# One ones product per norm, named activation tables, one-column bank marks, and another order at the ends of the feed-forwards and in the gated mixing

## The reference

```python
def rmsnorm(x, g):                       # called for every norm
    y = x * lax.rsqrt(jnp.mean(x * x, axis=-1, keepdims=True) + EPS)
    return y * g

def conv_ffn(h, w_up, conv_w, conv_b, w_down):        # ffn0
    up = jnp.pad(h @ w_up, ((0, 0), (1, 1), (0, 0)))
    u = sum(up[:, j:j + t] * conv_w[j] for j in range(3)) + conv_b
    a, g = jnp.split(u, 2, axis=-1)
    return (jax.nn.gelu(a) * g) @ w_down

def swiglu_ffn(h, w_in, w_out):                       # ffn1 to ffn4
    gate, up = jnp.split(h @ w_in, 2, axis=-1)
    return (jax.nn.silu(gate) * up) @ w_out

def gmlp_chunk_mix(h, w_uv, v_norm, w_s, b_s, w_o):   # mix2
    u, v = jnp.split(jax.nn.gelu(h @ w_uv), 2, axis=-1)        # 2048 wide each
    v = rms_norm(v, v_norm).reshape(B, 2, 128, 16, 128)        # 2 chunks, 16 groups
    sv = einsum('gts,bcsgd->bctgd', causal(w_s), v) + b_s      # a 128x128 product per group and chunk
    return (u * sv.reshape(B, S, 2048)) @ w_o

# first block: h = norm(x) @ w_in -> hgrn2 scan (two directions, with log of a sigmoid),
#   neighbourhood attention, attention on mem; gated sum @ w_out; conv_ffn; norm
# second block: ffn1, rwkv7, xattn, ffn2, ffn3, gmlp mix2, xattn, ffn4, final norm
```

## Time and profile before

| | before |
|---|---|
| median of 3 runs | 1980.64 us |
| the profiled execution's own time | 1974.38 us |
| its span (first to last instruction) | 1972.2 us |
| TensorE busy | 1886.9 us, 96% |
| TensorE weight loads | 1786.0 us, 91% |
| VectorE busy | 1407.4 us, 71% |
| ScalarE busy | 1044.1 us, 53% |
| GpSimd busy | 45.7 us, 2% |
| read from memory | 310.5 MB, 158 GB/s over the span |

### The profile page before, as it was taken

One profiled execution on the slowest core, in us unless ns is written; L12 is line 12 of the kernel. 1 busy time (PEld: TensorE's weight loads), 2 busy tenths in 40 slices (PEclk: granted clock), 3 DMA queues, 4 the chain that ended last, 5 costly groups with the idle time before them and its releaser, 6 DMA issues. The chain is left out here.

```text
span 1972.2 us, 40546 instructions
## 1 busy us (share of the span) xinstructions
PE 1886.9 (96%) x16839; PEld 1786.0 (91%) x16844; DVE 1407.4 (71%) x1786; ACT 1044.1 (53%) x1390; POOL 45.7 (2%) x42
## 2 busy tenths in 40 slices
PE   7999998999999999989987999999999998999998
PEld 7998997999998899989886999998999998999997
DVE  6685589767777877798565667778777756557776
ACT  6565576755556444568533554445444555545443
POOL 0000000000000000000052000000000000000000
PEclk9999999999999999999999999999999999999999
DMA  6843333354553455444401434554455453534552
GB/s 219 251 175 127 129 129 113 128 187 172 190 192 139 160 195 188 171 146 149 154 4 46 150 127 173 191 189 174 172 190 192 168 190 117 182 113 174 189 192 107
DMA packets 52316, 313.39 MB, mean 159 GB/s; under 512 B 13536, under 2 KB 13792, under 8 KB 14944
## 3 DMA queue, kind: packets, MB, share of 16 engines
q1 hardware_dynamic: 51760, 308.42, 44.2%
q10 hardware_dynamic: 432, 3.15, 0.4%
HBM read 310.50 MB, written 1.05 MB: 158 GB/s over the span
## 5 line engine op out<-in xcount | busy, mean ns | idle before, releaser
L2138 DVE TENSOR_TENSOR wl<-raw,wh 128x1024 fp32r<-128x1024 f32 x576 | 687.5, 1223 | 375.7 <-ACT wh L1462 372.8
L1462 ACT ACTIVATE wh<-raw 128x1024 fp32r<-128x1024 f32 x575 | 587.8, 1051 | 304.2 <-PE ps L308 154.8
L308 PE MATMUL ps<-pages_r,wh 128*128 128x256 f32 x2480 | 548.1, 287 | 34.1 <-DVE wl L2138 17.7
L308 PE MATMUL ps<-pages_r,wl 128*128 128x256 f32 x1680 | 479.0, 285 | 0.0
L308 PEld LDWEIGHTS ps<-pages_r,wh 128*128 128x128 f32 x2480 | 424.8, 195 | 38.8 <-issue 19.1
L308 PE MATMUL ps<-norm_r,wh 128*128 128x256 f32 x2336 | 430.2, 285 | 2.5 <-DVE norm_r L2202 1.7
L308 PEld LDWEIGHTS ps<-norm_r,wh 128*128 128x128 f32 x2336 | 365.9, 192 | 5.6 <-issue 2.0
L372 PE MATMUL ps<-norm_r,wh 128*128 128x512 f32 x1408 | 355.1, 394 | 2.6 <-DVE wl L2138 1.7
L308 PE MATMUL ps<-norm_r,wl 128*128 128x256 f32 x1184 | 335.0, 283 | 0.0
L308 PEld LDWEIGHTS ps<-pages_r,wl 128*128 128x128 f32 x1680 | 326.1, 194 | 0.0
L372 PEld LDWEIGHTS ps<-norm_r,wh 128*128 128x128 f32 x1408 | 253.5, 189 | 50.4 <-DVE wl L2138 2.4
(11 more groups left out here) (345 smaller groups left out, 1823.8 us busy)
## 6 DMA issues: line engine op xcount, KB each, us to landing
raw<-in_stream SPq DMA_DIRECT2D x287, 1024.0 KB, 4.8
pages<-in_rpb SPq DMA_DIRECT2D x32, 64.0 KB, 6.3
pages<-in_mem SPq DMA_DIRECT2D x2, 512.0 KB, 6.4
raw<-in_stream SPq DMA_DIRECT2D x2, 512.0 KB, 8.4
x<-in_x SPq DMA_DIRECT2D x1, 1024.0 KB, 12.3
pages<-in_mem ACTq DMA_DIRECT2D x1, 1024.0 KB, 5.0
pages<-in_gmlp_b ACTq DMA_DIRECT2D x1, 1024.0 KB, 4.5
pages<-in_gmlp_w ACTq DMA_DIRECT2D x1, 1024.0 KB, 6.6
```

What stands on the lines that cost most here:

```text
L308: mm = pe.matmul(out, left, right, start=start and q == 0, stop=stop and q == 2, skip_group_check=True)
L1462: f(t.wh[(2 * b0 + hf) % PIECE_SLOTS][:], t.raw[b0 % 2][:, hf * 1024:(hf + 1) * 1024], ACT.Copy).then_inc(s["high_done"], 1)
L2138: tt(t.wl[i][:], t.raw[b0 % 2][:, hf * 1024:(hf + 1) * 1024], t.wh[i][:].bitcast(F32), ALU.subtract).then_inc(s["low_done"], 1)
```

## The change

It has five parts.

- Norms. VectorE adds the second half's partial sum to the first (`made`, one more 128x256 add per norm), and `norm_sum` makes one product instead of two. `mem` and `mix2`, which also need the sums with tokens on the partitions, make two 128x1 products instead of four (of each half, two token blocks).
- Table sets. ScalarE names the set with both Ln and Exp ahead of the places where these stand (`preload_act_table_set`): in `norm_root`, `joint_root`, the scan's `log`, the group norms, the RWKV decay and mix2. The call puts a load in the program at its place.
- Bank marks. The zero products of a feed-forward write one column instead of 512.
- Ends of the feed-forwards. In the last written-out pair, ScalarE and VectorE take the gate's scaling and activation of the last step ahead of the first block's high and low parts; VectorE also puts one low half between making the hidden tile and taking its rest (`between`).
- Gated mixing. `gm_u` is cut to 2 blocks, and the other 6 blocks of u become `gm_w`, behind `gm_v`. The eight quarters stand behind the blocks of `gm_w`, by `MIX_BEHIND`: quarters 0 and 1 behind the second block, 2 behind the third, 3 and 4, then 5 and 6, then 7. ScalarE and VectorE are written in the same order.

The diff, cut to its core (further calls of `preload_act_table_set` are left out, as is the same edit for `mem` as for `mix2`):

```diff
@@ -90,11 +90,12 @@
-    ("ffn2", 44, 33), ("ffn3", 44, 33), ("gm_u", 8, 8), ("gm_v", 8, 8), ("gm_o", 4, 8),
+    ("ffn2", 44, 33), ("ffn3", 44, 33), ("gm_u", 2, 2), ("gm_v", 8, 8), ("gm_w", 6, 6), ("gm_o", 4, 8),
 WOVEN = 18
+MIX_BEHIND = (0, 1), (2,), (3, 4), (5, 6), (7,)
@@ -416,10 +417,8 @@
         parts, bank = norm_partial(t, name), 6 if name == "mem2" else 4
-        for hf in range(2):
-            pe.wait_ge(s["norm_part"], 2 * NORM[name] + hf + 1)
-            mm = pe.matmul(ps[:, bank, 0:T], cst(t, "ones"), parts[:, hf * T:(hf + 1) * T], start=hf == 0, stop=hf == 1)
-        mm.then_inc(s["norm_sum"], 1)
+        pe.wait_ge(s["norm_part"], 2 * NORM[name] + 2)
+        pe.matmul(ps[:, bank, 0:T], cst(t, "ones"), parts[:, 0:T], start=True, stop=True).then_inc(s["norm_sum"], 1)
@@ -466,7 +465,7 @@
         for bank in range(4, 8):
-            pe.matmul(ps[:, bank, :], t.zrow[:, :], t.zrow[:, 0:1].broadcast_to([P, 512]), start=True, stop=True,
+            pe.matmul(ps[:, bank, 0:1], t.zrow[:, :], t.zrow[:, 0:1], start=True, stop=True,
...
@@ -1128,17 +1125,19 @@
     pe.wait_ge(s["norm_part"], 2 * NORM["mix2"] + 2)
-    for hf in range(2):
-        for b in range(TB):
-            at_ = hf * T + b * P
-            pe.matmul(ps[:, 5, b:b + 1], norm_partial(t, "mix2")[:, at_:at_ + P], cst(t, "ones")[:, 0:1],
-                      start=hf == 0 and b == 0, stop=hf == 1, skip_group_check=True)
+    for b in range(TB):
+        pe.matmul(ps[:, 5, b:b + 1], norm_partial(t, "mix2")[:, b * P:(b + 1) * P], cst(t, "ones")[:, 0:1],
+                  start=b == 0, stop=True, skip_group_check=True)
     norm_sum("mix2")
-    project("gm_u", norm_parts, first=2, n=2)
-    project("gm_u", norm_parts, first=4)
     project("gm_v", norm_parts, groups=2, token=True)
-    pe.wait_ge(s["gm_mask"], 1)
-    for q in range(8):
+    def mix_quarters(qs):
+        for q in qs:
+            mix_pair(q)
+    def mix_pair(q):
@@ -1150,6 +1149,13 @@
         mm.then_inc(s["gm_mix"], 1)
+    project("gm_w", norm_parts, n=2)
+    pe.wait_ge(s["gm_mask"], 1)
+    mix_quarters(MIX_BEHIND[0])
+    for k in range(2, 6):
+        project("gm_w", norm_parts, first=k, n=1)
+        mix_quarters(MIX_BEHIND[k - 1])
...
@@ -1495,6 +1502,7 @@
     def norm_root(name):
+        act.preload_act_table_set("natural_log_exp_and_others")
@@ -1771,6 +1782,8 @@
     for q in range(4):
+        if q == 0:
+            act.preload_act_table_set("natural_log_exp_and_others")
...
@@ -1816,6 +1830,18 @@
                 step = (i * 2 + (1 + k), i * 4 + (2 + 2 * k), (1 + k) % 2, first and k == 0)
+                if k == 1 and isinstance(i, int) and i == trips - 1:
+                    early(*step)
+                    high(blk[0])
+                    if fi == 0:
+                        late(*step)
+                        high(blk[1])
+                        end(*step)
+                    else:
+                        high(blk[1])
+                        late(*step)
+                    high(blk[2])
+                    continue
...
@@ -2073,17 +2099,20 @@
     highs("gm_u", n=2)
+    act.preload_act_table_set("natural_log_exp_and_others")
     f(t.stat[:, 44:46], t.stat[:, 44:46], ACT.Exp, scale=-0.5).then_inc(s["gm_root"], 1)
-    for k in range(1, 9):
-        if 1 < k < 8:
-            high(BLK["gm_u"] + k)
-        c = slice((k - 1) * 512, k * 512)
-        act.wait_ge(s["u_evac"], SEG["gm_u"] + k)
+    def gate_gelu(k):
+        c = slice(k * 512, (k + 1) * 512)
+        act.wait_ge(s["u_evac"], (SEG["gm_u"] + k if k < 2 else SEG["gm_w"] + k - 2) + 1)
         f(t.pages[:, c], t.pages[:, c], ACT.Gelu_apprx_tanh).then_inc(s["gm_up"], 1)
+    gate_gelu(0)
+    gate_gelu(1)
@@ -2105,9 +2134,19 @@
         f(t.page[3][:, c], t.page[3][:, c], ACT.Copy, scale=t.stat[:, 35:36]).then_inc(s["gm_vout1"], 1)
-    for page in range(2):
-        operand_high(f"gm{page}", t.page[7 + page], t.page_r[10 + page],
-                     lambda q: act.wait_ge(s["gm_mixed"], 4 * page + q + 1))
+    def gated_high(q):
+        page, c = q // 4, slice(q % 4 * 512, (q % 4 + 1) * 512)
+        act.wait_ge(s["gm_mixed"], q + 1)
+        f(t.page_r[10 + page][:, c], t.page[7 + page][:, c], ACT.Copy).then_inc(s["op_high"], 1)
+    high(BLK["gm_w"])
+    gate_gelu(2)
+    for k, behind in enumerate(MIX_BEHIND):
+        high(BLK["gm_w"] + 1 + k)
+        gate_gelu(3 + k)
+        for q in behind:
+            gated_high(q)
@@ -2162,17 +2201,26 @@
+        parts = norm_partial(t, name)
+        def made(ins, hf):
+            if hf == 0:
+                ins.then_inc(s["norm_part"], 1)
+                return
+            link(ins)
+            tt(parts[:, 0:T], parts[:, 0:T], parts[:, T:2 * T], ALU.add).then_inc(s["norm_part"], 1)
             if name == "ffn1":
-                dve.tensor_reduce(norm_partial(t, name)[:, hf * T:(hf + 1) * T],
-                                  squares[:, at_:at_ + 1024].rearrange("p (k t) -> p t k", k=4), AX,
-                                  ALU.add).then_inc(s["norm_part"], 1)
+                made(dve.tensor_reduce(parts[:, hf * T:(hf + 1) * T],
+                                       squares[:, at_:at_ + 1024].rearrange("p (k t) -> p t k", k=4), AX,
+                                       ALU.add), hf)
             link(tt(squares[:, at_:at_ + 512], squares[:, at_:at_ + 512], squares[:, at_ + 512:at_ + 1024], ALU.add))
-            tt(norm_partial(t, name)[:, hf * T:(hf + 1) * T], squares[:, at_:at_ + T], squares[:, at_ + T:at_ + 2 * T],
-               ALU.add).then_inc(s["norm_part"], 1)
+            made(tt(parts[:, hf * T:(hf + 1) * T], squares[:, at_:at_ + T], squares[:, at_ + T:at_ + 2 * T], ALU.add), hf)
@@ -2529,12 +2577,13 @@
-    def hidden(fi, st, k, make):
+    def hidden(fi, st, k, make, between=lambda: None):
         make(t.work[:, k * 512:(k + 1) * 512])
+        between()
@@ -2577,14 +2626,22 @@
                 blk = [i * 6 + (r + j) if isinstance(i, int) else At(i * 6 + (r + j), r + j) for j in range(3)]
+                if k == 1 and isinstance(i, int) and i == trips - 1:
+                    early(i * 2 + 2, 0)
+                    low(blk[0])
+                    if fi == 0:
+                        step(i * 2 + 2, i * 4 + 4, 0)
+                        low(blk[1], (0,))
+                        end(i * 2 + 2, 0, lambda: low(blk[1], (1,)))
+                    else:
+                        low(blk[1], (0,))
+                        step(i * 2 + 2, i * 4 + 4, 0, lambda: low(blk[1], (1,)))
+                    low(blk[2])
+                    continue
                 step(i * 2 + (1 + k), i * 4 + (2 + 2 * k), (1 + k) % 2)
-                if fi == 0 and k == 1 and isinstance(i, int) and i == trips - 1:
-                    end(i * 2 + (1 + k), (1 + k) % 2)
-                    low(blk[2])
-                    continue
...
@@ -2937,23 +2994,18 @@
-        dve.wait_ge(s["piece_done"], 2 * (BLK["gm_u"] + k) + 2)
+        n, b = (SEG["gm_u"] + k, BLK["gm_u"] + k) if k < 2 else (SEG["gm_w"] + k - 2, BLK["gm_w"] + k - 2)
+        dve.wait_ge(s["piece_done"], 2 * b + 2)
         scaled(t.pages[:, k * 512:(k + 1) * 512],
-               ps[:, (SEG["gm_u"] + k) % BANKS, :].rearrange("p (n t) -> p n t", n=2), 2).then_inc(s["u_evac"], 1)
+               ps[:, n % BANKS, :].rearrange("p (n t) -> p n t", n=2), 2).then_inc(s["u_evac"], 1)
     gate_half(1)
-    lows("gm_u", 2, 1)
        ALU.mult).then_inc(s["gm_mask"], 1)
-    for k in range(2, 8):
-        gate_half(k)
-        if k < 7:
-            lows("gm_u", k + 1, 1)
     low_groups("gm_v", 0, 2)
-    dve.wait_ge(s["gm_up"], 8)
@@ -2967,7 +3019,8 @@
-    for q in range(8):
+    def mixed_quarter(q):
@@ -2976,10 +3029,19 @@
         link(ins)
+        dve.wait_ge(s["gm_up"], q + 1)
             mixed_low(q - 1)
+    gate_half(2)
+    lows("gm_w", 0, 1)
+    for k, behind in enumerate(MIX_BEHIND):
+        gate_half(3 + k)
+        lows("gm_w", 1 + k, 1)
+        for q in behind:
+            mixed_quarter(q)
...
```

25 lines of the change are left out of this document (13 added, 12 removed).

## The result

| | before | changed |
|---|---|---|
| median of the runs timed for the prediction | 1978.80 us (1976.13 to 1982.74, 4 runs) | 1950.21 us (1949.63 to 1951.46, 4 runs) |
| ratio, with its 95% interval | | 0.9855 (0.9835 to 0.9874) |
| the profiled execution's own time | 1974.38 us | 1950.35 us |
| span | 1972.2 us | 1948.6 us |

A forecast was written before the change was run, and what follows sets the result against it. TensorE, busy 96% of the span, was taken as the bound, so its removed work and waits count. Terms summed to 28.5 us: 1945.9 against the profiled execution, 1952.1 against the median; forecast 1951 us, range 1940 to 1964.

The forecast's parts named there:

- ffn1 with the ends of ffn1 to ffn4: Feed-forwards: table loads removed in ffn1 give 1.4 us; waits for the hidden low half go whole, 3.8 us.
- the gated mixing: In mix2, gm_w blocks hide the wait for v's norm and the slow quarters: 5.4 + 3.4 = 8.8 us.
- rival A: Gated mixing: VectorE's and TensorE's rounds are close, so part comes back; gain 10 to 20 us, 1961 to 1971; chance 0.15.
- B: Gated mixing: the ring between engines closes, 15.7 us a round against 7.2; full price 2003 us; chance 0.03.
- E: Whole kernel: no change, TensorE's removed time turns into waits for weights' low halves everywhere; chance 0.03.
- The marks: Feed-forward starts: one-column bank marks at 0.11 us instead of 0.22, 0.44 per feed-forward, 1.8 us in all.
- The load that is added: First projections: four table loads for the logarithms where there was one; cost 1.7 us, bounds 0 and 2.6.
- Rival C: Logarithms in the first projections: reloading the same set is free, 1.7 us better, 1949; counted within the forecast's 0.70.
- 4 to 5 us less time: Table loads: at the skill page's 2.66 us a switch, the estimate would be this much lower; by the rows not.
- The term of 2.5: End of ffn0: shorter wait for the hidden low half, 1.2 us, and full clock behind it, 1.3; bounds 0.5 and 4.5.
- VectorE work added: Twelve norms: one more 0.43 us add each, covered by the block under way; cost 0, up to 5 us without cover.
- Rival D: Mix1 and after the RWKV: shorter waits also spare TensorE half clock, 1.5 us per stretch; 1938 to 1945; chance 0.09.

The follow-up runs named there:

- e8: The kernel before with the new order at the feed-forwards' ends alone: 1971.48 us, 0.9972.
- e7: The kernel before with the gated mixing's new order alone: 1967.98 us, 0.9954.
- e5: The kernel before with the joined partial sums of the norms and the one-column bank marks alone: 1968.95 us, 0.9963.
- e6: The kernel before with all the named table sets alone, the four in the logarithms too: 1971.41 us, 0.9969.
- e9: The changed kernel with all eight mixed quarters behind the last block of gm_w, none between its blocks: 1954.82 us, 0.9892.
- e11: The kernel of e3 once more, without a further edit: 1949.07 us, 0.9861.
- e2: The kernel before, unedited, profiled once more: 1974.23 us, the profiled execution alone.
- e10: The kernel of e3 with the memory norm's partial sums again in two products of ones, without VectorE's added sum: 1951.37 us, 0.9876.
- e1: The changed kernel, unedited, profiled once more: 1950.13 us, 0.9866.
- e3: The changed kernel with the table set of the first projections' logarithms named once, not in each of the four: 1947.13 us, 0.9850.

## Why the prediction was right

**Right, with its mechanism and size.** The start (2.2 forecast, 2.0 measured), ffn1 with the ends of ffn1 to ffn4 (waits gone whole in e8), the RWKV keys (1.4 and 1.4), the RWKV's end (1.3 and 1.4), the final norm (1.3 and 1.3), and the gated mixing (8.8 and the ones product make 9.2; 9.4 measured, 9.0 alone in e7). The durations by which VectorE's round stayed under TensorE's held: no wait stands between gm_v and gm_o. Rivals A and B fall with that, E by e5. For rival A the prediction counted five waits on VectorE in the mixing before; the trace has two among the quarters, of 0.14 and 0.89 us.

**The marks were mis-sized.** Each was put at 0.11 us, from a 128x1 row of float32 products, against 0.22 before. Four take 0.12 us together, and a feed-forward gains 0.68 us, not 0.44. The term "4 x 0.44 = 1.8" measured 4 x 0.68 = 2.7.

**The load that is added** was put at 1.7, with bounds 0 and 2.6; the stage says 2.9 in the first pair and 2.5 in the second. The mechanism is as forecast (1.25 us of wait for block 15, 0.35 at the attention's first maximum). The other 0.8 us is a half-clock stretch that is not the load's, as e6, e7, e9 and e11 show; without it the loads cost 1.0 to 1.8 us, as priced. Rival C is refuted: the load at 113.11 repeats the set in place and takes 1.28 us. The Trainium skill, ScalarE: Activation LUTs, What ACT_TABLE_LOAD costs, gives its price for every switch to a different set; the trace shows that a load of the set in place is paid as well. Of the drain of about 1380 ns nothing is seen here either: the logarithm at 114.40 begins 1.29 us after its load. The "4 to 5 us less time" that the prediction worked out from that price does not follow from its own terms: with 7.8 us gained and 1.7 lost by loads, doubling both would give 6 to 7 us.

**ffn0 failed in two steps.** The term of 2.5 was 1.2 for the wait and 1.3 for the clock; 0.3 came out, under its lower bound of 0.5. The wait did fall by 1.1 us. But "with a shorter stand I expect full clock" was wrong: after 2.06 us of standing the clock is still at half for 3 us. Nor was the longer stand enough to bring half clock: the second trace of before (e2) stands 3.17 us at this place and then has full clock, and its ffn0 takes 182.48 us, 1.3 less. e9, which has the changed kernel's program up to mix2, stands 2.07 us and has full clock too (181.94 us, 1.5 less than the changed kernel). TensorE's row and the window behind it in e2, then the window in e9:

```profile
609.70 0.39 PE L308 MATMUL ps<-pages_r,wh 128*128 128x256 f32 x1 [3.01 <-DVE work_r L2540]
609.60:612.60 3.00, 2.90 (x24) 2.90 (x25) 2.92 (x4) 0.00 (x0) 0.00 (x0) 1.00 0.00 0
...
608.60:611.60 3.00, 3.00 (x26) 3.00 (x27) 2.70 (x3) 0.86 (x2) 0.00 (x0) 1.00 0.79 273
```

In all, half clock follows in four of the five traces with the long stand and in eight of the nine with the short one. So the price of 1.3 us was right, but no run shows that the change could earn it: it falls out differently in executions of one program. And "VectorE work added: cost 0, the cover is the second half of the block under way" failed at one of twelve norms, the memory's, where the added sum stands ahead of low halves. In the changed kernel it is 0.33 us of wait and 0.17 at the block behind, 0.5 together (e5 and e10).

**The clock elsewhere** gave 1.5 us in mix1 in the first pair and 0.9 after the RWKV. Rival D forecast such gains from shorter waits. In mix1 the traces do not bear it out: e5, in which nothing inside mix1 is changed, has one half-clock stretch less than before and takes 78.58 us against 80.10, while e1, with the shorter wait, has as many as before (78.79 us). Behind the RWKV the stretch is 3.4 us long in six of the eight traces of the whole change and 6.8 in the other two and in all six others, e6 with the same shorter wait among them. So it is not a gain to count on.

**The RWKV scan had no term**, and should have had a bound: 5 us either way. It is what separates the sum (28.5) from the traces (24.0); the terms that came out too high (ffn0, the logarithms) and those that came out too low (marks, the clock in mix1 and after the RWKV) nearly cancel. That the time came out within 1 us of 1951 is therefore luck in part. It is owed to the choice between the profiled execution and the median: the profiled one of before, 1974.4, had the shortest scan of all fourteen traces, so that 28.5 off it was too low, and 28.5 off the median slightly too high.

## What to carry to other kernels

Where one engine is busy 96% of the span, count the work removed from it first, and then each wait with the engine that ends it; here the parts added up within what runs and traces can tell. A table set is worth naming once ahead of a wait, and never in a helper that is called in a row, since a load of the set in place costs as much as any. When time is gained in front of a stage, look again at when the transfers there start and land: 1 us of the logarithms' gain was lost to a 1 MB transfer that began 1.9 us later behind its issue and ran into the next block's, and moving its issue by 18 us brought it back. And have two traces of before: here the second would have shown that the half clock behind ffn0 comes and goes, and a stretch like the RWKV scan, which differs between them, needs a bound of its own in the sum.

## What the runs showed of the hardware

- Whether half clock follows a stand of TensorE is not settled by the length of the stand alone. At the end of ffn0 a stand of 2.06 us was followed by 3 us at half clock (0.54 in the window from 609.3) and one of 2.07 us in e9 by full clock; one of 3.18 us by half clock in before and one of 3.17 us in e2 by full clock. The stretches at half move from execution to execution of one kernel: near 311 us in the second trace of before and not in the first, at 866 in e1 and not in the changed kernel's first trace.
- A bf16 product of 128x1 follows the next after 0.03 us; a float32 one takes 0.11 us a row, and a product is two rows.
- A 1 MB transfer of ScalarE's queue began 2.8 to 3.0 us behind its issue instead of 1.0 in e3, e10 and e11, and then ran 3.6 to 3.7 us, as elsewhere. SyncE's block, issued with 2.6 us of it still to run, landed after 6.7 to 7.1 us instead of 4.9.
- In a chain of 64x64 products between engines TensorE's idle time lies between 14.4 and 18.2 us at the same work (14.4 to 16.0 in thirteen of fourteen traces), about half of it with no releaser in the profile. Each 3.4 us at half clock there make it busy 1.5 us longer on average.
